# Expert weights stored by expert and partition, loaded in long rows

## The reference

```
def expert_block(args):
    xblk, ex = args
    h = jax.nn.silu(xblk @ w_gate[ex]) * (xblk @ w_up[ex])
    return h @ w_down[ex]

y_slot = ...                      # rows of the blocks, back in token order
return einsum("tkd,tk->td", y_slot, wts)
...
u = x * (1.0 + scale2) + shift2
y_moe = _hier_moe(u, w_rg, w_re, w_e_gate, w_e_up, w_e_down)
x = _layer_norm(DEEPNORM_ALPHA * x + gate2 * y_moe, ln_g[1], ln_b[1])
```

## Time and profile before

| | |
|---|---|
| time, median of 3 runs | 1943.59 us (1940.41 to 1945.24) |
| the profiled execution: its own time, its span | 1941.17 us, 1939.4 us |
| granted TensorE clock, mean | 0.948 |
| PE busy | 1767.9 us, 91% |
| DVE, ACT, POOL busy | 59%, 32%, 31% |
| all transfers | 342.76 MB, mean 177 GB/s |
| expert phase, first weight load to last down product | 1245.4 to 1814.7 us of the span |

### The profile page before, as it was taken

How to read it: one execution, slowest core, us unless ns; L and a number is a source line. 1 busy time by engine, 2 the same in 40 slices (tenths; PEclk the granted TensorE clock), 3 DMA queues, 4 the chain that set the end, 5 groups by cost and what they waited for, 6 DMA issues and landing times. The chain is left out here.

```text
span 1939.4 us, 29471 instructions
## 1 busy us (share of the span) xinstructions
PE 1767.9 (91%) x9156; PEld 1379.9 (71%) x9157; DVE 1144.8 (59%) x1864; ACT 617.2 (32%) x770; POOL 596.8 (31%) x685
## 2 busy tenths in 40 slices
PE   5999999999999999999689988549999999999674
PEld 3888788888888899999568777337766677766431
DVE  3566655565666765566476778744465333455298
ACT  2333322223333222222121111115555434455233
POOL 0122221012222222022035455534344333344155
PEclk7999999999999999999799999669999999999887
DMA  8544344434333222331466343378899765798595
GB/s 254 151 131 123 97 137 131 131 116 131 99 94 97 82 78 77 100 92 59 124 210 195 120 143 108 120 255 278 296 361 373 266 232 172 254 316 292 201 394 180
DMA packets 301930, 342.76 MB, mean 177 GB/s; under 512 B 18932, under 2 KB 257300, under 8 KB 299391
## 3 DMA queue, kind: packets, MB, share of 16 engines
q1 hardware_dynamic: 278726, 284.30, 45.7%
q0 software_dynamic: 18000, 55.87, 8.0%
q10 hardware_dynamic: 5106, 1.31, 0.4%
HBM read 276.86 MB, written 64.58 MB: 176 GB/s over the span
## 5 line engine op out<-in xcount | busy, mean ns | idle before, releaser
L1534 DVE TENSOR_TENSOR w_gu_lo<-w_gu_raw,w_gu_hi (+1 forms) x64 | 146.4, 2291 | 154.5 <-ACT w_gu_hi L1527 148.1
L658 POOL TENSOR_TENSOR o_r<-o_ms,neg_half 128x4 f32<-128x4 f32 (+1 forms) x16 | 16.8, 1052 | 662.9 <-DVEq L932 662.9
L896 DVE TENSOR_TENSOR w_lo<-w_raw,w_hi 128x1024 fp32r<-128x1024 f32 x112 | 138.2, 1237 | 139.4 <-ACT w_hi L546 136.7
L1874 PE MATMUL ph<-w_gu_hi,x_hi 128*128 (+1 forms) x408 | 179.8, 441 | 11.7 <-DVE hh L1783 9.3
L713 PE MATMUL pr<-ub_hi,w_hi 128*128 128x288 f32 (+1 forms) x672 | 189.2, 335 | 0.0
L713 PE MATMUL pr<-ub_hi,w_lo 128*128 128x288 f32 (+1 forms) x672 | 184.2, 328 | 0.0
L713 PE MATMUL pr<-ub_lo,w_hi 128*128 128x288 f32 (+1 forms) x672 | 183.6, 327 | 0.0
L713 PE MATMUL pr<-ua_hi,w_hi 128*128 128x512 f32 x448 | 183.2, 409 | 0.0
L1913 PE MATMUL py<-w_dn_w,hhT 128*128 x400 | 180.7, 594 | 0.1
L713 PE MATMUL pr<-ua_lo,w_hi 128*128 128x512 f32 x448 | 177.6, 396 | 0.0
L713 PE MATMUL pr<-ua_hi,w_lo 128*128 128x512 f32 x448 | 177.5, 396 | 0.0
(11 more groups left out here) (337 smaller groups left out, 3494.1 us busy)
## 6 DMA issues: line engine op xcount, KB each, us to landing
w_raw<-in_w_in SPq DMA_DIRECT2D x112, 512.0 KB, 4.1
w_gu_raw<-in_w_e_gate SPq DMA_DIRECT2D x32, 1024.0 KB
w_gu_raw<-in_w_e_up SPq DMA_DIRECT2D x32, 1024.0 KB
w_dn_w<-in_w_e_down SPq DMA_DIRECT2D x32, 1024.0 KB
w_mod<-in_w_mod SPq DMA_DIRECT2D x16, 1024.0 KB
y_t<-y_scratch SPq DMA_DIRECT2D x16, 1024.0 KB, 7.6
w_ring<-in_w_mod SPq DMA_DIRECT2D x4, 2048.0 KB, 17.5
x_cols<-in_x_prompt SPq DMA_DIRECT2D x32, 256.0 KB, 5.4
```

The lines of the kernel that those rows point to most:

```text
L658: pool.tensor_tensor(o_r[:, 0:c], o_ms[:, 0:c], keep["neg_half"][:, 0:c], ALU.pow).then_inc(o_rs, 1)
L896: dve.tensor_tensor(w_lo[:, n % WS], w_raw[:, n % WRAW], w_hi[:, n % WS].bitcast(F32), ALU.subtract).then_inc(lo_done, 1)
L1534: dve.tensor_tensor(w_slot(keep["gu_lo"], s, lo, hi), w_slot(keep["gu_raw"], r, lo, hi), w_slot(keep["gu_hi"], s, lo, hi).bitcast(F32), AL ...
L1874: last = pe.matmul(ph[:, :], x[:, half, k * P:(k + 1) * P], w_slot(w, s, k * GU, (k + 1) * GU), start=(k == 0 and m == 0), stop=(k == KT - ...
```

## The change

The host lays the expert weights out anew ahead of the launch. Gate and up become one array `w_e_gate_up`, (32, 128, 4096): for each expert and each partition, all that this partition's row of `gu_raw` holds, 16 KB in one piece. `w_e_down` becomes (32, 128, 2048), 8 KB for each expert and partition. SBUF holds the same numbers in the same places as before. `load_gate_up` issues one transfer of 128 rows of 16 KB in place of two of 1024 pieces of 1 KB, and `load_down` one of 128 rows of 8 KB in place of 256 pieces of 4 KB. The semaphores `wg_in` and `wu_in` become one, `wgu_in`.

```diff
-def gate_up_w(buf, s):
-    return buf[:, bass.ds(s, 1), 0:KT * 2 * DE].rearrange("p a (k c f) -> p (a k) c f", k=KT, c=2)
-
 def load_gate_up(eng, io, keep, e, s):
-    for c, (w, landed) in enumerate((("w_e_gate", "wg_in"), ("w_e_up", "wu_in"))):
-        eng.dma_start(gate_up_w(keep["gu_raw"], s)[:, :, c, :],
-                      io[w][0, bass.ds(e, 1)].rearrange("e (k p) f -> p (e k) f", p=P)).then_inc(keep[landed], 16)
+    eng.dma_start(w_slot(keep["gu_raw"], s, 0, 2 * KT * DE),
+                  io["w_e_gate_up"][bass.ds(e, 1)].rearrange("e p w -> p (e w)")).then_inc(keep["wgu_in"], 16)
...
 def load_down(eng, io, keep, e, s):
-    eng.dma_start(keep["dn_w"][:, bass.ds(s, 1), :].rearrange("p a (k n) -> p (a k) n", k=DE // P),
-                  io["w_e_down"][0, bass.ds(e, 1)].rearrange("e (k p) n -> p (e k) n", p=P)).then_inc(keep["wd_in"], 16)
+    eng.dma_start(w_slot(keep["dn_w"], s, 0, DE // P * D),
+                  io["w_e_down"][bass.ds(e, 1)].rearrange("e p w -> p (e w)")).then_inc(keep["wd_in"], 16)
...
                 def gate_up(e, s):
...
-                    for landed in (wg_in, wu_in):
-                        wait_apart(sp, landed, 16 * e, tick)
+                    wait_apart(sp, wgu_in, 16 * e, tick)
                     load_gate_up(sp, io, keep, e, s)
...
+def lay_out(inputs):
+    a = {name: np.asarray(value) for name, value in inputs.items()}
+    gate, up = (a.pop(n)[0].reshape(NE, KT, P, DE) for n in ("w_e_gate", "w_e_up"))
+    a["w_e_gate_up"] = np.concatenate((gate, up), axis=3).transpose(0, 2, 1, 3).reshape(NE, P, KT * 2 * DE)
+    a["w_e_down"] = a["w_e_down"][0].reshape(NE, DE // P, P, D).transpose(0, 2, 1, 3).reshape(NE, P, DE // P * D)
+    return a
```

More of the change, by code:

```diff
@@ L1555, in expert_phase @@
     gu_hi, gu_lo, dn_w, gu_l = keep["gu_hi"], keep["gu_lo"], keep["dn_w"], keep["gu_l"]
-    wg_in, wu_in, wd_in = keep["wg_in"], keep["wu_in"], keep["wd_in"]
+    wgu_in, wd_in = keep["wgu_in"], keep["wd_in"]
     KD = DE // P
@@ L1642, in _ @@
                     if e:
-                        for landed in ("wg_in", "wu_in", "wd_in"):
+                        for landed in ("wgu_in", "wd_in"):
                             sp.wait_ge(keep[landed], 16 * e)
@@ L1721, in split_gu @@
                     if a == 0:
-                        act.wait_ge(wg_in, 16 * e + 16)
-                        act.wait_ge(wu_in, 16 * e + 16)
+                        act.wait_ge(wgu_in, 16 * e + 16)
                     if last is not None:
@@ L2291, in build @@
                 keep[name] = ectx.enter_context(nc.sbuf_tensor("w_" + name, [P, slots, width], dt))
-            for name in ("wg_in", "wu_in", "wd_in", "gu_h", "gu_l"):
+            for name in ("wgu_in", "wd_in", "gu_h", "gu_l"):
                 keep[name] = ectx.enter_context(nc.semaphore(name))
@@ L2303 @@
     arrays, args = {}, {}
-    for name, value in inputs.items():
+    for name, value in lay_out(inputs).items():
         a = np.ascontiguousarray(value)
```

## The result

The changed kernel is slower: 1966.2 us (median of 4 runs, 1960.9 to 1968.3) against 1944.0 of the kernel before beside it; the ratio is 1.0115, with a 95% interval of 1.0094 to 1.0136. Forecast were 1934 us and a range up to 1946. The profiled execution took 1960.94 us, 19.8 more than that of before.

A forecast was written before the change was run, and what follows sets the result against it. The PE's pace was taken as the bound, except in slow stretches waiting on the scatter and at the start. Gains of 6.8 + 3 = 9.8 us off 1941.2 gave 1931.4, on the median's footing 1934 us; range 1927 to 1946.

The forecast's parts named there:

- What bounds the kernel: Expert loop: loses 13.6 us against the PE's pace, mostly in two slow stretches, where ACT and POOL wait for the scatter.
- The rate: Weight loads: 414 GB/s for long rows against 359 for 1 KB packets; a slow block's transfers take 10.1 us, not 10.9.
- The step that failed: Slow stretches: the block period was taken as 10.5 us against 11.05, half of the loss won.
- a chain of 9.2 and one of 12.8 us: Slow stretches: best and worst case per block, the scatter's landing after 6.4 or 10.0 us plus 2.79 for the rest.
- the term of 6.8 us won: Expert loop, slow stretches: gain expected from a shorter wait for the scatter, called the softest number.
- the skill's rule: Queue sharing: an engine drains a packet of 9 to 17 descriptors before switching, so 2.1 MB would pass in 5.1 us.
- The best case's first part: Scatter's wait: the same 1.65 MB stand ahead of it and pass at 414 GB/s in 4.0 us.
- Elsewhere nothing is to be had: Expert loop outside the two slow stretches: no gain expected, since blocks there run at the PE's pace of 10.01 us.
- The start: Before block 0: faster first loads, list and gather win 3 us, bounds 0 (list falls behind the third load) and 5.
- The slower one: Rival: scatter stands behind whole 16 KB pieces, also outside the slow stretches; period 11.9, 12 us more, 1952.6 us; chance 0.13.
- the three that were to show the prediction wrong: Profile after: intervals of 11 us or more with DMA engines resting; new intervals above 10.01; block 0's list after the third load.
- The rate of 400 GB/s: Sign for the forecast: DMA rate in the slow stretches at 400 GB/s or above, with a share below 1.

The follow-up runs named there:

- two slots on the kernel before: Kernel before, with two slots for y_sb and ids_cur; POOL waits for the previous scatter only ahead of the next one: 1933.2 us, ratio 0.9956.
- the kernel with two of each: Changed kernel with two slots for y_sb and ids_cur, two scatters and two gathers on their way, output without the experts: 1928.9 us, ratio 0.9923.
- the 4 KB kernel: Kernel before, with gate and up in one transfer of 4 x 128 pieces of 4 KB, down still in 4 KB pieces: 1943.9 us, ratio 1.0014.
- The holding run: 4 KB pieces for gate, up and down, two slots of y_sb and ids_cur, expert 2's load held until block 0 is gathered: 1929.3 us against 1932.4 without hold.

## Why the prediction was wrong

**What bounds the kernel** was read rightly: two slots on the kernel before take 10.4 of the 13.6 us away, by the link that the earlier trace rows name first.

**The rate** was right as a property and worth nothing as a term. The 408 GB/s of the kernel with two of each stand beside the 414 that were taken. But the period of the slow stretch was 8.26 + 2.79 us, issue to landing and the rest of the chain, and the landing did not come sooner with the rate. In the 4 KB kernel the long pieces are there, a scatter takes 8.5 us on the mean (before 8.1), and the period stays at 11.0.

**The step that failed** is "I take 10.5 us, half way between the PE's 10.01 and today's 11.05". The ends worked out just before it were a chain of 9.2 and one of 12.8 us, with their middle at 11.0; and since no block is shorter than 10.01, the middle of what was possible was 11.4. The choice took the PE's pace as one end and today's period as the other, which shut out every loss from a term whose worst case was a loss of 1.8 us a block. Measured were 11.46 us in those eight blocks, so the term of 6.8 us won was a loss of 20.2 in the loop. Two sentences ahead stood the true mechanism, eight pieces of the scatter against as many of 8 or 16 KB; its price did not enter the term. It follows from rows: eight turns of 16 KB are 128 KB for each engine, 2.1 MB for all, 5.1 us at 414 GB/s (the figure that the prediction gives under the skill's rule only) in place of 0.52 MB and 1.3 us. That is up to 3.8 us more for a scatter, if the load lasts so long. The trace shows 1.56 MB and 5.4 us for the scatter that had most of a load beside it. The best case's first part failed too: the wait ahead of the scatter was to fall from 4.6 to 4.0 us and was 4.3, at 1.46 MB.

Under the choice lay a misreading of the earlier trace rows: q1's 174 packets were taken for pieces of 1 KB, and the sharing for one "by packets, not by bytes". They hold 3 KB each on the mean, and with pieces of 1 KB alone nearly four pass for one of 4 KB (495 beside 130). So today's sharing was even in bytes, and a piece of 16 KB could only tip it against the scatter.

**Where it acts** was the second error. "Elsewhere nothing is to be had" is true of gains and was used for losses. By the chain of the earlier trace rows, where block after block waits for a landing, one of 10.01 us hides a landing of 10.01 - 2.79 = 7.2 us. One late landing by itself can be absorbed, as the 11.4 us of 1561.63 show, but with 16 KB rows too many are that late. Of the 20.2 us, 7.9 were added outside the two slow stretches, where before 0.3 us were lost and the prediction looked for nothing, and 12.3 inside them, where it looked for a gain.

**The start**, 3 us won, came out near its named lower bound, 0, and for the reason named there: the list fell behind the third load. Two faster loads gained 2.2 us, not the 4 expected. The list was issued only 0.9 us sooner after the first load and took 4.8 us more, the gather 1.8 less (7.2 from 1276.20), and the first transposes of hh came 0.7 us later, which is no difference that can be told. The holding run shows that the order of issue there is worth 5.3 us, more than any rate.

**The rivals.** The slower one was right in its mechanism and place, and held 0.13. Its price of 12 us is what the two slow stretches came to, 12.3. It named the loss outside them and gave it no price, 7.9 us, and it took off 3 us for a start that won nothing; so its 1952.6 was still 13.6 us short. The skill's rule that led there (the Trainium skill, DMA: Bandwidth & Descriptors, section on queues, rings and completion order) was set aside since the rows show equal sharing. Its packet of 9 to 17 descriptors is not what the traces show with 16 KB pieces either, 104 of q1 beside 139 of q0. Nor did the trace agree with it for the 4.6 us in which q0 got nothing, as the prediction has it: 1615 pieces are about 100 for each of the 16 engines. A further line of the same page of the Trainium skill, in the section on SWDGE, HWDGE and iDMA, calls a packet preferably at most 4096 B and the boundary at which an engine changes queues. It stands there for transfers that POOL issues, but the counts of q1 fit it too: nearly four pieces of 1 KB for one of the scatter, one piece where they are longer, and next to no loss up to 4 KB.

**The signs.** Two of the three that were to show the prediction wrong came, intervals above 10.01 where there were none and a list that lands after the third load. The third came in half: 11.46 us, but with engines at rest for little of it (a share of 0.98). The rate of 400 GB/s did not come (367).

**Open** stays why some 1.5 MB of q1 pass before the first piece of a scatter, at 1 KB as at 16 KB. The opposite test, a scatter with shorter or longer rows of its own, was not run, and neither was the layout of before with two scatters and two gathers on their way. So it is not shown that long rows are worth anything even then; with two slots alone 1 KB pieces left 3.2 us.

## What to carry to other kernels

Ask of a transfer change first whether the path holds its bytes or somebody's latency: here a loop waited for a small indirect transfer, and faster neighbours did not shorten that wait. When a bulk queue shares the engines with one that somebody waits for, its pieces should be no longer than those of the other (here 4 KB); or let two of the short transfers be on their way, after which long rows cost the loop nothing here. And if a cost is bounded on both sides, take the middle of those bounds, not of the bound and today's value, and look for it also in the blocks that lose nothing today. Before a row is used to tell pieces from bytes, divide its bytes by its pieces.

## What the runs showed of the hardware

- Before the first piece of a scatter issued beside a long load, q1 moved 1.65 MB in 4.6 us with 1 KB pieces and 1.46 MB in 4.3 us with 16 KB; only the second part, the sharing, grew, from 2.5 to 5.4 us. With nothing on q1 (scatter of 1532.69) no packet moved for the first 1.5 us either, and all 0.52 MB had passed 3.1 us after the issue.
- Sharing of one engine pool by two queues: beside pieces of 4 KB nearly four of 1 KB passed for one (495 beside 130), and at most one of 16 KB (104 beside 139).
- A read of 2 KB on q0, issued 0.40 us behind a load of 3 MB in long rows, took 6.8 us. With one load of 1 KB pieces nearly done ahead of it, it took 2.0 (1271.62 to 1273.61).
- The Trainium skill (Perfetto Trace Analysis, section on DMA optimizations) says that going from 2 KB to 4 or 8 KB for a transfer can raise throughput much when a kernel is bound by DMA. The DMA share of 1.05 in the earlier trace rows looks like that case. No gain in time followed at 4 KB, and 8 KB lost 0.8%. With the waits out of the way the rate did rise, from 372 to 408 GB/s, in part because the same nine blocks then took 90.1 us and not 97.7.
